# A fixed table of ranks sets the order of thirteen experts in a two-layer mixture-of-experts kernel

## What is computed

```
scores = sigmoid(t @ w_router); sel = scores + router_bias
# the best of 4 groups of 4 experts, then the best two experts in it
hid = silu(x @ w_gate[e]) * (x @ w_up[e])     # e_gate, e_up: 1024 x 512
y   = hid @ w_down[e]                          # e_down: 512 x 1024
h   = layer_norm(alpha * h + g2 * sum_k weight_k * y_k)
```

| | expert 0, 1, 2 | experts 3 to 15 | blocks of 0, 1, 2 | blocks of the others, fullest first (rank 0 to 12) |
|---|---|---|---|---|
| layer 0 | 62, 25, 57 | 72 125 63 130 252 44 33 11 36 31 46 23 14 | 2, 1, 2 | 8 5 4 3 2 2 2 2 2 1 1 1 1 (sum 34) |
| layer 1 | 19, 47, 19 | 27 25 150 101 252 117 73 37 13 1 72 29 42 | 1, 2, 1 | 8 5 4 4 3 3 2 2 1 1 1 1 1 (sum 36) |

## Time and profile before

### The profile page before, as it was taken

How to read it: one execution, slowest core, us unless ns; L and a number is a source line. 1 busy time by engine, 2 the same in 40 slices (tenths; PEclk the granted TensorE clock), 3 DMA queues, 4 the chain that set the end, 5 groups by cost and what they waited for, 6 DMA issues and landing times.

```text
span 1218.7 us, 36590 instructions
## 1 busy us (share of the span) xinstructions
PE 1073.9 (88%) x15056; PEld 664.2 (54%) x15057; DVE 534.0 (44%) x1510; ACT 207.8 (17%) x555; POOL 179.0 (15%) x229
## 2 busy tenths in 40 slices
PE   3899989999799889999877489999998899998876
PEld 0444444445444477877666344444445787776652
DVE  0236653446316754444333371304467444444327
ACT  1222243334212100000000151101220000000010
POOL 0001200000000021222111250410002222222121
PEclk9899999999899899999998799999989999999888
DMA  8932289998142469599999776116063969999964
GB/s 316 383 124 88 84 291 349 325 377 345 59 116 109 173 265 417 223 420 417 421 420 418 254 251 236 69 69 241 35 240 129 419 236 418 415 422 420 420 233 172
DMA packets 97183, 329.72 MB, mean 271 GB/s; under 512 B 15561, under 2 KB 28273, under 8 KB 88817
## 3 DMA queue, kind: packets, MB, share of 16 engines
q1 hardware_dynamic: 65632, 288.98, 60.6%
q10 hardware_dynamic: 25168, 20.71, 5.5%
q0 software_dynamic: 6336, 19.41, 4.4%
HBM read 312.27 MB, written 25.18 MB: 277 GB/s over the span
## 4 chain that ended last, share of the span: by engine, by line
PE 61%; DMA 19%; DVE 9%; issue 3%; SPq 3%; ACT 2%; ACTq 1%; POOL 0%; POOLq 0%; DVEq 0%
PE PS L1460 15%; PE PS L1470 9%; DMA ring<-in_e_down_dram 9%; PE PS L1286 8%; PE PS L1535 8%; PE PS L1387 7%; PE PS L1307 4%; PE PS L1216 3%; DMA RFW<-in_e_down_dram 3%; DMA expert_rows<-RE 3%; PE PS L1318 2%; DVE mx L870 2%; DMA ring<-in_w_ada_dram 2%; DMA fold_rows<-fsh 1%; SPq L337 1%
## 5 line engine op out<-in xcount | busy, mean ns | idle before, releaser
L1460 PE MATMUL PS<-ring,RE 128*32 128x128 f32 x7040 | 210.4, 279 | 32.0 <-DMA ring<-in_e_up_dram 18.2
L1460 PEld LDWEIGHTS PS<-ring,RE 128*32 128x32 f32 x7040 | 201.9, 113 | 45.3 <-issue 40.4
L1470 PE MATMUL PS<-ring,RE 128*32 128x256 f32 x1760 | 115.9, 382 | 6.1 <-DMA ring<-in_e_down_dram 3.0
L682 ACT ACTIVATE RE<-PS 128x64 f32<-128x64 f32 x160 | 35.7, 223 | 472.8 <-PE PS L1460 435.3
L1387 PE MATMUL PS<-ring,UR 128*128 128x512 f32 x256 | 112.9, 595 | 1.9 <-ACT G L643 1.1
L1127 DVE TENSOR_TENSOR RE<-RE,PS 128x64 f32<-128x64 f32 x160 | 35.4, 221 | 177.6 <-ACT RE L682 177.6
L1535 PE MATMUL PS<-ring,UR 128*128 128x512 f32 x256 | 110.8, 593 | 2.6 <-ACT UR L724 2.6
L1460 PE MATMUL PS<-UR,RE 128*32 128x128 f32 x3072 | 95.2, 283 | 10.8 <-DMA UR<-in_e_up_dram 8.5
L1460 PEld LDWEIGHTS PS<-UR,RE 128*32 128x32 f32 x3072 | 91.1, 114 | 15.8 <-issue 12.8
L1286 PE MATMUL PS<-ring,UR 128*128 128x512 f32 x224 | 98.4, 593 | 0.7 <-ACT UR L571 0.7
L482 POOL DMA_INDIRECT RE<-tokens,gcol x80 | 79.6, 996 | 60.3 <-POOL gcol L496 60.3
(11 more groups left out here) (257 smaller groups left out, 1105.6 us busy)
## 6 DMA issues: line engine op xcount, KB each, us to landing
ring<-in_w_ada_dram SPq DMA_DIRECT2D x24, 2048.0 KB, 11.5
ring<-in_e_down_dram SPq DMA_DIRECT2D x22, 2048.0 KB, 28.4
ring<-in_e_gate_dram SPq DMA_DIRECT2D x22, 2048.0 KB, 19.2
ring<-in_e_up_dram SPq DMA_DIRECT2D x22, 2048.0 KB, 23.4
UR<-in_e_up_dram SPq DMA_DIRECT2D x10, 2048.0 KB
RFW<-in_e_down_dram SPq DMA_DIRECT2D x10, 2048.0 KB
UR<-in_e_gate_dram SPq DMA_DIRECT2D x10, 2048.0 KB
expert_rows<-RE ACTq DMA_DIRECT2D x320, 32.0 KB
```

The costliest lines, as they stand in the source:

```text
L682: A(gs[:, 64 * h:64 * h + 64], PS[:, h, 0:64], ACT.Silu).then_inc(silu_rd[l], 1)
L1460: ins = mm(PS[BLK * q:BLK * q + BLK, h, 0:P].rearrange("p (g b i) -> p g b i", g=2, b=2), xT[:, k, :], wgu[:, :, k, 2 * h:2 * h + 2, q, :] ...
L1470: ins = mm(PS[BLK * q:BLK * q + BLK, 5, 0:256], hidT[:, BLK * k:BLK * k + BLK], wd[:, k, 256 * q:256 * q + 256], start=(k == 0), stop=(k = ...
```

## The change

The position of an expert no longer comes from a formula but from a table of thirteen ranks: position s3+i takes the expert of rank TURNS[i]. Thirteen one-column memsets at the head of DVE's program write the table into `rank_at`; the two instructions that made `epos` are gone, and `perm` compares the rank with the table.

```diff
+TURNS = (3, 6, 2, 8, 5, 1, 7, 4, 9, 0, 10, 11, 12)
...
-        epos = sb("epos", [P, NF])
+        rank_at = sb("rank_at", [P, NF])
...
+            assert sorted(TURNS) == list(range(NF))
+            for f, r in enumerate(TURNS):
+                ins = V_.memset(rank_at[:, f:f + 1], float(r))
+            link(ins)
...
-                link(V_.tensor_scalar(epos[:, :], erank[:, :], -2.0, float(2 * NF - 1), ALU.mult, ALU.add))
-                link(V_.scalar_tensor_tensor(out=epos[:, :], in0=erank[:, :], scalar=2.0, in1=epos[:, :], op0=ALU.mult,
-                                             op1=ALU.min))
-                link(V_.tensor_tensor(perm, epos[:, :].unsqueeze(2).broadcast_to([P, NF, NF]),
-                                      iota_s[:, 0:NF].unsqueeze(1).broadcast_to([P, NF, NF]), ALU.is_equal))
+                link(V_.tensor_tensor(perm, erank[:, :].unsqueeze(2).broadcast_to([P, NF, NF]),
+                                      rank_at[:, :].unsqueeze(1).broadcast_to([P, NF, NF]), ALU.is_equal))
```

## The result

The changed kernel takes 1215.47 us, median of 4 runs (1212.88 to 1215.85), against 1228.61 (1227.09 to 1230.1) for the kernel before, measured with it: ratio 0.9885, 95% interval 0.9866 to 0.9905. That is 13 us (1.1%) faster where 24.5 were forecast, and 1.5 us above the range of 1196 to 1214. The profiled execution took 1212.88 us by its own time, with a span of 1211.0.

A forecast was written before the change was run, and what follows sets the result against it. Early expert blocks were taken as PE-bound, later ones as load-bound after an unrecovered 14 us DMA gap. Gains 11.7 (layer 0), 12.0 (layer 1) and 0.8 (DVE instructions) sum to 24.5: 1229.2 − 24.5 = 1204.7 us, range 1196 to 1214.

The forecast's parts named there:

- the account of the loads: Expert stages: without the early DMA gap, loads stream from 490 and 987; PE ends at 668.8 and 1165.8 us.
- Prices: Expert stages: a block costs 5.45 to 5.6 us, taken as 5.55 beside full DMA, 5.5 in the tail; a load 17.1.
- PE without any wait: Expert stages from s3 on, no waits for weights: ends at 655 and about 1162, an upper gain of 43 us, 1186.
- The gain forecast for layer 1: Layer 1's expert stage ends at 1165.8 instead of 1177.9, gain 12.0 us, with PE the limit almost throughout.
- I carry that distance over: Whole kernel: the runs' median lies 8.8 us above the profiled execution, added unchanged, giving 1204.7 us.
- at nothing, at most 2 us: Behind layer 0's experts: three DMAs, about 3 MB and 7 us, wait behind s15's load, ending at about 674.
- s15's load: End of each stage: issued only when s12 ends, on idle DMA, 2 + 15 us plus about 1 for the blocks' rows.
- Rival 3: End of each stage: s15's load is bared; at 28.4 us the change starts to cost, at 30 1231 us; chance 0.03.
- Rival 1: Expert stages: PE starved earlier, s15 late; loads of 18 instead of 17.1 us, gain about 12, 1217; chance 0.12.
- Rival 2: Expert stages: PE becomes the limit because loads take 16.3 instead of 17.1 us; gain about 32, 1197; chance 0.15.
- Rival 4: Expert order does not matter: it is not the table's, or the tail loses the time; within 0.2%, chance 0.03.
- cross-check of layer 0: Layer 0's stage: load stream starts 66.4 us sooner, PE's rest grows 51.1, gathers and stores cost 3.6: gain 11.7.

The follow-up runs named there:

- plain: Both kernels with a plain load in place of POOL's indirect gather in the block loop: changed 1197.51 us, kernel before 1218.74 us.
- d_new_direct: Changed kernel with plain loads in place of POOL's indirect gathers in the block loop, rows not the reference's: 1197.51 us, ratio 0.9718.
- a_oldorder: Changed kernel's code with the old order in its table, so only the code differs from the kernel before: 1230.59 us, ratio 1.0009.

## Why the forecast was right and wrong

The table shows six profiled executions in us: PE's time from s0's first product to the end of s15's last, and what lies ahead, between and behind. "First" is the pair of profiles first shown, "again" the second pair, "plain" the pair with the plain load.

| | head | layer 0 | between | layer 1 | behind | span |
|---|---|---|---|---|---|---|
| before, first | 428.1 | 252.5 | 250.0 | 247.4 | 40.8 | 1218.7 |
| changed, first | 425.1 | 245.8 | 251.9 | 249.8 | 38.5 | 1211.0 |
| before, again | 428.8 | 259.3 | 250.7 | 252.4 | 38.1 | 1229.3 |
| changed, again | 428.6 | 245.9 | 251.7 | 250.0 | 38.1 | 1214.2 |
| before, plain | 427.4 | 252.8 | 250.4 | 246.3 | 38.2 | 1215.1 |
| changed, plain | 428.0 | 240.2 | 251.6 | 235.9 | 39.8 | 1195.5 |

**Right: the account of the loads.** The forecast's ends, 668.8 and 1165.8, are 240.7 and 235.3 us after s0 began in the earlier trace rows's execution (at 428.09 and 930.53). The plain pair, where a block is 5.44 us, gives 240.2 and 235.9. (In layer 1 that pair routes a little differently, since its rows do; the 40 blocks stay.) The wait of s8 for its down weights was 2.10 us for a forecast 2.0. PE stood idle 6.59 us before s12, loop turn included, where the forecast has 1.6 for the turn and 7.4 behind it: the weights came at 602.45 for a forecast 603.8, and PE was a little later. The row of 6.44 for the block after a long wait was the nearer guide: 6.03 here, at a granted clock of 0.60, and not the 7.4 of a wholly cold block that I had worked out beside the Trainium skill (TensorE: Matmul & The Clock Gate, Part 1). The stages together gain 12.6 + 10.4 = 23.0 for 23.7.

**Wrong: the step "Prices".** I took 5.45, 5.55 and 5.5 us for a block. In every profile with the indirect gather and the full products, but the first, it is 6.0. The forecast's own bound "PE without any wait" shows what that does. With 6.0 in place of 5.5 it comes to 461.8 + 34 x 6.0 + 6.4 = 672.2 and 957.7 + 36 x 6.0 + 6.4 = 1180.1, which is 244.1 and 249.6 us after s0; measured are 245.8 and 249.8. PE is the limit in both layers and the loads wait for it. The gain forecast for layer 1, 12.0, is the term that this undid. The kernel before loses less by the same 0.55 us a block, 259.3 − 252.5 = 6.8 and 252.4 − 247.4 = 5.0, because its late blocks wait for weights anyway. The changed one loses about 5.7 and 14.1 (its rows "again" against "plain"). So for the forecast's 11.7 and 12.0 the pair "again" shows 13.4 and 2.4: at 6.0 us a block, layer 1 of the kernel before (252.4) was already near PE's own pace (249.6).

**Wrong: "I carry that distance over".** The profiled execution was 8.8 us below the median. I treated this as a constant to add. It was the price of a stall in PE's stream which that execution lacked and which the change makes dearer. The plain pair shows the size of the error: 21.2 us of gain without the stall, 13 to 15 with it.

**Not refuted: the tail "at nothing, at most 2 us".** Between the stages, where s15's load and the three DMAs behind it end later than before, the changed kernel loses 1.9, 1.0 and 1.2 us in the three pairs. PE stood idle 16.30 us for the gathered rows behind layer 0 in the first profile of the changed kernel, and 14.79 in the second of the kernel before. Behind layer 1 the pairs go either way (−2.3, 0.0, +1.6), and one kernel's own profiles differ there by 2.7 (40.8 and 38.1), so nothing can be read from it.

**s15's load**: gate issued at 1151.42, and the down product began on its weights at 1170.61, after a wait of 0.63 us: 19.2 us for a forecast 18.0. In d_new_direct, layer 0, it was 647.05 to 666.26, 19.2 again. This is PE's timeline of the changed kernel at that place:

```profile
1170.61 1.93 PE L1477 MATMUL PS<-ring,RE 128*32 128x256 f32 x32 [0.63 <-DMA ring<-in_e_down_dram]
```

Rival 3 needed 28.4. Rival 1's time, 1217, is near the one measured, but by luck: it came from slower loads. Rival 2 named the right limit, PE, but from faster loads and at 1197; none of the rivals had a slower PE. Rivals 1 and 4 did not happen: in layer 0 no load is waited for between s6 and s12, and the order alone carries the whole gain (a_oldorder).

**Two slips in the working** change little. In the cross-check of layer 0 the gathers and stores of 5 blocks are priced at 3 us and subtracted as 3.6; with 3 it gives 12.3 in place of 11.7. And s15's down weights land 16.1 us after the end of s12 in layer 0 and 16.8 in layer 1, for the same load.

**The DVE instructions** are off the chain as said, worth 0.8 us at most and not seen: the head alone varies from 425.1 to 428.8 between profiles.

## What to carry to other kernels

When weights stream through a few banks, an item with much work holds its bank for long. Put a few middling ones first, so that the stream starts at once, and the fullest late enough that the loads have run ahead but early enough that its work still covers the last ones; then ask what limits next, because that limit's price decides how much is kept. If the one profiled execution is off the median by more than the effect of a per-iteration cost of a few tenths of a microsecond, count iterations times such a cost before carrying the distance over as a constant: here 80 blocks at 0.55 us could hold 44 us, of which 8.8 showed.

## What the runs showed of the hardware

An indirect DMA issued by POOL (0.98 us there) makes PE's stream break just as it ends and costs a block of 5.44 us about 0.55. In most blocks PE waits for nothing that the profile names ("issue"); in 17 of the changed kernel's 80 (20 in its second profile) the wait is put down to DVE's transposition, which the break itself has made late. It does so with full and with light load traffic at a fully granted clock, follows the gather when that is moved, and costs the same with 64 rows as with 128. A plain DMA from POOL in its place (0.54 us) does not do it. Twelve profiles with these gathers and the full products show it, eleven of them on four chips (for the changed kernel's first the chip is not on record), with the pause at 64 to 77 of 75 to 82 gathers in each; one, the first of the kernel before, does not, with gathers of the same length at nearly the same place in the block. What set that execution apart stays open: the same program, profiled twice more, had the break both times, and the chip of that execution is not on record. I did not try to gather without an indirect DMA while computing everything, which would be the next step: by the plain load in the changed kernel it is worth up to 18 us on top of this change. Nor is it shown through what POOL's instruction holds PE up.
